# The MoE stage's up weights issued from ScalarE's queue behind the gate's tanh

## The reference, cut to what matters

```python
h = jax.nn.silu(jnp.einsum('nd,edf->nef', t, wg)) * jnp.einsum('nd,edf->nef', t, wu)
h = h * comb[:, :, None]
y = jnp.einsum('nef,efd->nd', h, wd)
```

## Time and profile before

| | us |
|---|---|
| median of 3 runs | 911.65 |
| lowest and highest run | 909.9 and 912.21 |
| the profiled execution | 912.9 |
| span of the profile | 911.0 |
| TensorE busy (matmul), VectorE, ScalarE | 800.2, 459.5, 250.9 |
| first `GU` starts | 624.0 |
| last `GU` starts | 874.9 |

### The profile page before, as it was taken

The page is one execution under the profiler, slowest core; times in us unless marked ns, Lnnn a source line. Parts: engine busy times, 40 slices in busy tenths (PEclk is TensorE's granted clock), DMA queues, the critical chain, the costliest instruction groups (busy, mean ns, idle before and its releaser), DMA issues.

```text
span 911.0 us, 16423 instructions
## 1 busy us (share of the span) xinstructions
PE 800.2 (88%) x6090; PEld 510.3 (56%) x6090; DVE 459.5 (50%) x1067; ACT 250.9 (28%) x585; POOL 66.7 (7%) x74
## 2 busy tenths in 40 slices
PE   3999999999999999999999799957997887877860
PEld 3566666666766666666667564444554554544530
DVE  2476586786785875867867644351111111111115
ACT  4223351441432423514414222321111111111102
POOL 1000000000000000000000000002332222222110
PEclk9999999999999999999999799956999999999995
DMA  9451060250230500602502206755999999999925
GB/s 222 105 145 25 24 170 9 59 140 23 77 98 23 155 20 23 169 7 57 140 23 63 100 26 228 283 218 177 347 393 399 396 398 402 400 391 398 391 80 193
DMA packets 112633, 159.31 MB, mean 175 GB/s; under 512 B 27232, under 2 KB 91290, under 8 KB 104394
## 3 DMA queue, kind: packets, MB, share of 16 engines
q1 hardware_dynamic: 96580, 148.62, 47.3%
q0 software_dynamic: 5296, 6.19, 2.4%
q10 hardware_dynamic: 10727, 4.09, 1.8%
HBM read 155.99 MB, written 13.64 MB: 186 GB/s over the span
## 4 chain that ended last, share of the span: by engine, by line
PE 69%; DMA 17%; DVE 9%; issue 2%; ACT 1%; ACTq 1%; DVEq 0%; SPq 0%; POOL 0%; POOLq 0%
PE bank L591 17%; DMA vecs<-in_exp_down 8%; PE bank L943 8%; DMA wall<-in_exp_down 4%; PE bank L597 4%; PE bank L864 4%; PE bank L950 4%; PE bank L745 4%; PE bank L808 3%; PE bank L693 3%; DMA scratch<-in_exp_down 2%; PE bank L613 2%; PE bank L937 2%; PE bank L700 2%; DVE vecs L1360 2%
## 5 line engine op out<-in xcount | busy, mean ns | idle before, releaser
L591 PE MATMUL bank<-xnT,wall 128*128 128x320 f32 x656 | 197.3, 446 | 1.8 <-DVE wkv L1466 1.8
L591 PEld LDWEIGHTS bank<-xnT,wall 128*128 128x128 f32 x656 | 120.1, 191 | 52.2 <-DVE wkv L1466 5.4
L1705 DVE SCALAR_TENSOR_TENSOR vecs<-vecs,bank 128x128 f32<-128x128 f32 x32 | 9.2, 287 | 160.0 <-ACT vecs L1249 160.0
L943 PE MATMUL bank<-scratch 128*64 128x256 f32 x512 | 58.8, 382 | 19.0 <-DMA scratch<-in_exp_down 9.6
L943 PEld LDWEIGHTS bank<-scratch 128*64 128x64 f32 x512 | 40.3, 137 | 33.0 <-issue 19.8
L1699 DVE COPY vecs<-bank 128x512 f32<-128x512 f32 x32 | 22.1, 691 | 64.1 <-PE bank L950 64.1
L1249 ACT ACTIVATE vecs<-bank 128x128 f32<-128x128 f32 x32 | 8.9, 277 | 148.3 <-PE bank L943 148.3
L497 POOL DMA_INDIRECT merged<-xn2d,gidx x2 | 1.9, 942 | 613.6 <-DVE sidx L1693 613.3
L745 PE MATMUL bank<-xnT,wall 128*128 128x320 f32 x128 | 43.9, 455 | 2.5 <-DVE wkv L1506 2.5
L1459 DVE TENSOR_TENSOR wkv<-bank,consts_sb 128x256 f32<-128x256 f32 (+1 forms) x40 | 18.1, 451 | 48.4 <-PE bank L693 48.4
L943 PE MATMUL bank<-vecs,scratch 128*64 128x256 f32 x256 | 32.3, 409 | 8.8 <-DMA vecs<-in_exp_down 6.5
(11 more groups left out here) (374 smaller groups left out, 1376.1 us busy)
## 6 DMA issues: line engine op xcount, KB each, us to landing
wall<-in_w_in SPq DMA_DIRECT2D x58, 512.0 KB, 5.5
vecs<-in_exp_down SPq DMA_DIRECT2D x16, 1024.0 KB, 18.7
scratch<-in_exp_gate SPq DMA_DIRECT2D x16, 1024.0 KB, 16.0
scratch<-in_exp_up SPq DMA_DIRECT2D x16, 1024.0 KB, 20.3
vecs<-in_exp_gate SPq DMA_DIRECT2D x8, 1024.0 KB, 15.5
vecs<-in_exp_up SPq DMA_DIRECT2D x8, 1024.0 KB, 19.9
scratch<-in_exp_down SPq DMA_DIRECT2D x8, 1024.0 KB, 18.3
wall<-in_exp_gate SPq DMA_DIRECT2D x8, 1024.0 KB, 16.3
```

The costliest lines, as they stand in the source:

```text
L591: q = mm(tpbank(L, name), wbuf[name][:, k, :], xnT[:, k, :], start=(k == 0), stop=(k == KC - 1))
L943: q = mm(b[64 * f:64 * f + 64, 0:256], xT[:, k, :], w[:, :, k, 128 * f:128 * f + 128], start=(k == 0), stop=(k == KC - 1))
```

## The change

The up weights of experts 4 to 31 are no longer issued by SyncE but by ScalarE, on its own queue, right behind the tanh of expert e-4. Gate and down weights stay on SyncE's queue with their waits. Each expert's three transfers count on the same semaphore as before. The first four experts' weights, and the extra ones for overflowing experts, are still issued by SyncE.

```diff
+        def gu_src(name, e):
+            return a[name][0].rearrange("e (p k) f -> p e (k f)", k=KC)[:, bass.ds(e, 1), :].rearrange("p e x -> p (e x)")
...
             def weights(j, e, sem, before=None):
                 if before is not None:
                     sp.wait_ge(S("gu"), before)
                 for g, name in enumerate(("exp_gate", "exp_up")):
-                    sp.dma_start(wgu[j][:, g].rearrange("p k f -> p (k f)"), gu_src(name, e)).then_inc(S(sem), 16)
+                    if before is None or g == 0:
+                        sp.dma_start(wgu[j][:, g].rearrange("p k f -> p (k f)"), gu_src(name, e)).then_inc(S(sem), 16)
                 if before is not None:
                     sp.wait_ge(S("dn"), before)
                 sp.dma_start(wdn[j], dn_src(e)).then_inc(S(sem), 16)
...
                     A(th, bank[2 + j % 2][:, 0:128], ACT.Tanh, scale=0.5).then_inc(S("th"), 1)
+                    if not last:
+                        act.dma_start(wgu[j][:, 1].rearrange("p k f -> p (k f)"), gu_src("exp_up", i * 4 + (j + 4))).then_inc(S(f"ew{j}"), 16)
```

More of the change, by code:

```diff
@@ L350, in hawk_rwkv7_moe, with dn_src @@
         w_in = a["w_in"][0].rearrange("(k p) n -> p k n", p=P)
+        def gu_src(name, e):
+            return a[name][0].rearrange("e (p k) f -> p e (k f)", k=KC)[:, bass.ds(e, 1), :].rearrange("p e x -> p (e x)")
+        def dn_src(e):
+            return a["exp_down"][0].rearrange("e (j p) d -> p e j d", p=P)[:, bass.ds(e, 1)].rearrange("p e j d -> p (e j) d")
         @block.sync
@@ L431, in _ @@
             sp.dma_start(norm2b, a["norm2"].broadcast_to([P, D])).then_inc(S("x1_in"), 16)
[L433 to L437, removed]
             def weights(j, e, sem, before=None):
```

## The result

| | before | changed |
|---|---|---|
| median of 20 runs, us | 912.37 | 915.75 |
| lowest and highest | 909.57, 914.33 | 912.25, 920.03 |
| ratio, with its 95% interval | | 1.0043 (1.003 to 1.0056) |
| profiled execution, span | 912.9, 911.0 | 915.4, 913.6 |

The change costs 3.9 us by the ratio (2.7 to 5.1). The time lies in the predicted range of 908.5 to 917.5, but on the slower side of the 0.3% bound, to which the prediction gave 0.35, and 2.5 us above the predicted 913.2.

The account below looks back on a forecast made before the run. Weight transfers were taken to bound the expert stage, 8.585 us per expert against TensorE's 6.76. Issues 0, hole -2.2, middle 0 and end +3.7 moved the last `GU` by +1.5 us: 911.65 + 1.5 = 913.2 us, range 908.5 to 917.5.

Parts of the forecast that it names:

- Issues: Expert stage: removing 28 issues from SyncE gives 0; adding them to ScalarE between tanh and copy costs 0.
- The hole at the beginning: DMA engines run dry from 637 to 641 us; ScalarE's early up 5 fills this, -2.2 us.
- The middle: Steady part of the expert stage: only the landing order changes, the period stays 8.585 us, 0.
- Rival D: Expert stage: two queues raise the transfer rate, saving 7.6 us, time 905.6; chance 0.13.
- The end: Experts 28 to 31: loads land 5.3 us apart, TensorE needs 6.76, so the last `GU` lags them by 3.7 us.
- rival B: From expert 28 on, TensorE's clock falls after waits, 1.7 us each: 914.9 with one, 916.6 with two; chance 0.18.
- C: Expert stage: ups on ScalarE's queue get under 0.29 of the rate and land last, 917 us; chance 0.09.
- A: Expert stage: loads land in order of issue, only the beginning's hole is filled, -2.2 us, 909.4; chance 0.12.

Follow-up runs that it names:

- the middle alone: Against the kernel before, ScalarE issues only the ups of experts 8 to 27, SyncE all others: 916.49 us, ratio 1.0039.
- the kernel without the end: Against the kernel before, ScalarE issues the ups of experts 4 to 27, SyncE those of 28 to 31: 913.91 us, ratio 1.0008.
- the end alone: Against the kernel before, ScalarE issues only the ups of experts 28 to 31, SyncE all others: 918.81 us, ratio 1.0063.
- the halved pair: Changed kernel and kernel before, gate and up of experts 28 to 31 summed over half their inputs: 911.84 us (0.9996) and 910.68 us (0.9986).
- the fillers: Changed kernel plus four unused 128x128 matmuls ahead of each wait for weights of experts 4 to 27: 916.28 us, ratio 1.0042 to the kernel before.
- the first ups alone: Against the kernel before, ScalarE issues only the ups of experts 4 to 7: 908.67 us, ratio 0.9955; run a second time, 0.9972.

## Why the prediction was off by 2.5 us

**Issues: right.** SyncE's 28 issues gave nothing, ScalarE's cost nothing; they lie in the 0.74 us that the copy waits for TensorE anyway.

**The hole at the beginning, -2.2: right in kind, a little too large.** It is filled. Alone it brought 1.0 to 1.5 us by the ratios on SyncE's queue (their intervals reach from a gain of 2.8 us to none), 1.2 to 1.8 in the profiles. The forecast read 2.2 us from the mean share of the 16 DMA engines, while the landing is that of the slowest; that this makes the difference wasn't tested.

**The middle, 0: this step failed.** The prediction held that order alone changes, that the backlog never empties and that the period stays. In the profile of the changed kernel the stream shows it: the last down landed at 874.96, where 872.65 was forecast and 874.85 was measured before; from the start of `GU` 0 that is 0.6 us earlier than before, not 2.2. The bytes per time fall by about 1%, and the middle alone costs 3.6 us (1.9 to 5.2), of which its profile shows 1.8. The backlog does run out at times, behind a long wait and a slow `GU`: 1.8 us unused in the kernel without the end, 2.5 in the end alone. In the changed kernel the share fell to 0.71 and 0.48 in the two microseconds from 855 on, behind `GU` 27. With the beginning it comes to +0.7, where -2.2 was forecast. The two don't quite add (-1.5 and +3.6 against 0.7), within their intervals; both kernels also switch back to one queue at expert 28, and the middle alone switches to two at expert 8, which the changed kernel doesn't. So how much the middle costs in the changed kernel is known only roughly; its stream's end, 1.6 us less gained than forecast, is the nearest figure. Rival D is out: two queues moved 393 to 396 GB/s from 680 to 800, one queue 397 to 399. The rule of the Trainium skill that I cited for it (DMA: Bandwidth & Descriptors, section Issuing engines are not separate DMA queues) is that issuing from several engines saves only the time to issue; the runs agree in that no bandwidth was gained. Why the rate is lower while the share is as high stays open. The mixing of two queues' loads and the less even waits of the experts are both possible; no run tells them apart.

**The end, +3.7: right in kind and nearly in size.** TensorE doesn't keep up behind the last loads: 3.2 us by the kernel without the end, 3.0 by the halved pair, 4.3 in the profile with a fall of the clock in it (2.8 without, by the estimate above), 3.3 in the profile with the fillers. The kernel with the end alone lost more, 5.7 us, with the dry stretch in it. Downs 29 to 31 landed at 864.2, 869.6 and 874.96, 5.3 us apart for the last two, as worked out. Two details were wrong. With the end alone the lag starts at expert 27, since three ups pass its down; in the changed kernel down 27 took the usual 17.7 us. And the fall of the clock (rival B) came there at `GU` 27, ahead of the point where I let it count. It counted all the same: at full clock TensorE would have waited for downs 28 and 29, with the fall it was late for both and had no wait left to make it up.

**Sum.** Beginning and middle together +0.7 instead of -2.2, the end +3.2 instead of +3.7: +3.9 instead of +1.5. In the profile: the last load lands 2.3 us later than forecast, 0.7 of it because the stage began later, and the last `GU` comes 4.3 instead of 3.7 us behind it, at 879.23 instead of 876.35. The measured 915.75 lies above the forecast's own range of 911.2 to 914.8. It lies in the wider one because rivals B and C had stretched that upwards, and neither is what happened in the middle.

**Rivals A and C.** The order isn't kept (A), and ScalarE's queue isn't starved (C): its loads land in 9.9 us (median), gates and downs on SyncE's in 16 to 19.

## What to carry to other kernels

Where transfers are the bound and wait behind one another, a second queue added no room here. It decided who passes whom: what passed early was paid for by what landed last, and the price showed at the end of the stage, where the consumer got its inputs faster than it could use them. Where the issues themselves wait for the consumer, look also for what one long wait does to the stream behind it: the next issues come late, and the DMA engines can run dry. A hole in the stream can be filled by moving an issue ahead on the queue that there is. And let each consumer wait only for the transfers it reads: the wait of `GU` for down weights was worth 3.6 us in the changed kernel and 0.9 to 2.5 us with the first ups alone (3.2 to 3.5 in the profiles).

## What the runs showed of the hardware

With the up loads on a queue of their own, the 16 DMA engines moved 393 to 396 GB/s from 680 to 800 us, with one queue 397 to 399, at the same busy share of 1.01 or 1.02. A 1 MB load landed 28.0 us after its issue on the one queue, where its neighbours took 17 to 22: three loads issued on the other, from 2.9 us before it to 17.1 us after it, landed first, in 9.4 to 9.9 us each.
